# A chunked delta-rule scan in a DiT layer: whole Gram rows to memory, inverted blocks back in two transfers and spread on chip, key sums moved two chain steps up

## What is computed

```python
def update(s, w_t, k_t, v_t, kk_t, a_t):
    sa = jnp.einsum('ebhvk,ebhk->ebhv', s, kk_t)
    return s * w_t[..., None, :] - sa[..., :, None] * (kk_t * a_t)[..., None, :] + v_t[..., :, None] * k_t[..., None, :]

def rwkv_run_scan(s0, r, decay, k_dir, v, kk, a):
    ...
    s, y = wkv_scan(s0, per_dir(rw_heads(decay)), per_dir(rw_heads(k_dir)), shared(rw_heads(v)), shared(kk), per_dir(rw_heads(a)), rr)
    if y is not None:
        y = y[0] + jnp.flip(y[1], axis=1)
    return s, y
```

## Time and profile before

| | |
|---|---|
| median of three runs | 2519.59 us (2517.39 to 2519.63) |
| the profiled execution | 2521.18 us |
| its span in the profile | 2519.0 us |
| busy: PE, PEld | 2218.5 us (88%), 1843.3 us (73%) |
| busy: DVE, ACT, POOL | 938.4 us, 668.9 us, 877.0 us |
| DMA | 155526 packets, of which 103271 under 512 bytes |
| mean granted TensorE clock | 0.952 |

### The profile page before, as it was taken

How to read it: one execution, slowest core, us unless ns; L and a number is a source line. 1 busy time by engine, 2 the same in 40 slices (tenths; PEclk the granted TensorE clock), 3 DMA queues, 4 the chain that set the end, 5 groups by cost and what they waited for, 6 DMA issues and landing times. The chain is left out here.

```text
span 2519.0 us, 51099 instructions
## 1 busy us (share of the span) xinstructions
PE 2218.5 (88%) x22528; PEld 1843.3 (73%) x22528; DVE 938.4 (37%) x1467; ACT 668.9 (27%) x1027; POOL 877.0 (35%) x708
## 2 busy tenths in 40 slices
PE   5899989979699999999879996777777787999997
PEld 3787855655499999999729985666666665888785
DVE  3112265970500000122495126666666434000123
ACT  4111066421400000122222134444444313111112
POOL 2223200101143434434134454333333233666562
PEclk8999999989799999999889998999999988999998
DMA  6555520001022121121112342222222122232221
GB/s 254 204 209 193 216 93 18 1 34 50 17 67 67 58 66 58 58 68 59 44 67 75 105 145 55 45 46 45 45 45 43 27 73 80 95 97 92 92 92 67
DMA packets 155526, 205.64 MB, mean 82 GB/s; under 512 B 103271, under 2 KB 113767, under 8 KB 148168
## 3 DMA queue, kind: packets, MB, share of 16 engines
q1 hardware_dynamic: 155336, 202.78, 25.6%
HBM read 184.65 MB, written 18.09 MB: 80 GB/s over the span
## 5 line engine op out<-in xcount | busy, mean ns | idle before, releaser
L253 POOL CAST TMP_r<-WR 128x1024 fp32r<-128x1024 f32 x120 | 127.2, 1060 | 723.0 <-DMA WR<-in_ffn_w_dram 437.6
L272 PE MATMUL PS<-H_r,TMP_r 128*128 128x384 f32 (+1 forms) x1088 | 330.4, 359 | 11.0 <-DVE Y_r L489 11.0
L272 PE MATMUL PS<-Y_r,TMP_r 128*128 128x384 f32 (+1 forms) x1088 | 330.2, 358 | 3.7 <-DVE H_r L489 3.7
L255 POOL TENSOR_TENSOR WR_r<-WR,TMP_r 128x1024 fp32r<-128x1024 f32 x120 | 289.0, 2408 | 9.6
L412 DVE TENSOR_TENSOR P<-TMP,PS 128x768 f32 (+1 forms) x44 | 36.1, 821 | 562.5 <-PE PS L272 562.5
L272 PEld LDWEIGHTS PS<-H_r,TMP_r 128*128 128x128 f32 x1088 | 202.7, 190 | 27.5 <-DVE Y_r L489 11.7
L272 PEld LDWEIGHTS PS<-Y_r,TMP_r 128*128 128x128 f32 x1088 | 201.6, 190 | 19.3 <-DVE H_r L489 4.0
L272 PE MATMUL PS<-H_r,WR_r 128*128 128x384 f32 x736 | 191.9, 342 | 0.0
L395 ACT ACTIVATE TMP<-PS 128x768 f32<-128x768 f32 (+1 forms) x44 | 31.0, 705 | 526.0 <-PE PS L272 526.0
L589 PE MATMUL PS<-H_r,TMP_r 128*128 128x384 f32 x704 | 151.9, 338 | 3.2 <-DVE H_r L627 2.2
L272 PE MATMUL PS<-Y_r,WR_r 128*128 128x512 f32 x352 | 139.2, 396 | 0.0
(11 more groups left out here) (325 smaller groups left out, 4463.8 us busy)
## 6 DMA issues: line engine op xcount, KB each, us to landing
WR<-in_ffn_w_dram SPq DMA_DIRECT2D x88, 512.0 KB, 3.7
TMP<-in_mod_w_dram SPq DMA_DIRECT2D x40, 1024.0 KB, 5.0
WR<-in_down_dram SPq DMA_DIRECT2D x44, 512.0 KB, 3.5
WR<-in_mix_w_in_dram SPq DMA_DIRECT2D x24, 512.0 KB, 6.7
WR<-in_rw_w_rkv_dram SPq DMA_DIRECT2D x24, 512.0 KB, 4.4
P<-in_mod_w_dram SPq DMA_DIRECT2D x4, 2048.0 KB, 21.8
vkr_dram<-extra SPq DMA_DIRECT2D x16, 384.0 KB, 5.1
scan_front<-vkr_dram SPq DMA_DIRECT2D x16, 384.0 KB, 4.2
```

What stands on the lines that cost most here:

```text
L253: nc.gpsimd.tensor_copy(hi, raw).then_inc(weights_hi, 1)
L255: nc.gpsimd.tensor_tensor(lo, raw, hi.bitcast(F32), ALU.subtract).then_inc(weights_split, 1)
L272: last = nc.tensor.matmul(PS[:, bank + b, 0:h1 - h0], w, x[:, h0:h1], start=k + p == 0, stop=k == CT - 1 and p == 2)
```

## The change

1. Gram rows: 4 transfers (one for each direction and half of the partitions, whole rows of 64 values, 256 bytes) replace the 16 of L2109. They go to `gram_dram`, in which a chunk's matrix is followed by a gap of 64 values, so that the diagonal blocks of all 96 matrices lie at one stride; two transfers, one for each direction, read 16 values of each of 16 rows into each of 96 partitions.
2. Inverses: `XC` and `YC` come back dense, 128 partitions by 24 x 16 values, one transfer each. ACT spreads `XC` into the block-diagonal `XY` with 4 instructions whose scale is a column of `rowblock` (one for the partitions of that block, else zero), ahead of `ta`. DVE does the same for `YC`, 4 instructions ahead of `kin_0`. The fifth part still comes by 8 transfers, on a semaphore of its own. The solved rows and `XC`, `YC` share memory, so SP waits for `yt` of the round instead of for `tb`.
3. The sigmoid of the rate is no longer finished on POOL (`s01`, `s11` go): ACT reads the tanh, with the factor 0.5 moved into its column, and DVE adds 1 and multiplies by 0.5 within `ba` and `bt`, now scalar_tensor_tensor.
4. Order. PE: `kk` from between links 9 and 10 to between 7 and 8, `CK_0` and `KD_1` each one gap later, `kr` ahead of `CK_1`, `var` into the sweeps. ACT: `kc ksq` ahead of `tK_1`, `groot` ahead of `oo_0`, `vwide` ahead of `kT_0`. DVE: `kmax krec` between links 8 and 9, `m5` and `n_0` ahead of `f1 f2 z`, `kt_1` and `acc_1 accr` later in the chain, `kmul` ahead of the last masks.

```diff
-                        blocks = AM[:, n % 2, e].rearrange("p h j t -> p (h j) t")
                         for p in range(2):
-                            for b in range(4):
-                                at = 64 * p + BK * b
-                                sp.dma_start(blk_dram[e, :, p, b].rearrange("x s t -> s x t"),
-                                             blocks[at:at + BK, :, BK * b:BK * b + BK]).then_inc(blk_out, 16)
-                    sp.wait_ge(blk_out, 256 * n + 256)
-                    sp.dma_start(BLK.rearrange("q (e n) -> q e n", e=2),
-                                 blk_dram.rearrange("e x p b s t -> (x p b) e (s t)")).then_inc(blk_back, 16)
+                            sp.dma_start(gram_dram[e, :, p, 0:TC * TC].rearrange("x (s t) -> s x t", t=TC),
+                                         AM[H2[p], n % 2, e].rearrange("p h j t -> p (h j) t")).then_inc(blk_out[e], 16)
+                    for e in range(2):
+                        sp.wait_ge(blk_out[e], 32 * n + 32)
+                        diagonal = bass.AP(gram_dram.tensor, gram_dram[e].offset, [[BK * TC + BK, NBLK], [TC, BK], [1, BK]])
+                        sp.dma_start(BLK[:, BK * BK * e:BK * BK * (e + 1)].rearrange("q (s t) -> q s t", t=BK),
+                                     diagonal).then_inc(blk_back, 16)
...
-                        sp.wait_ge(pe_done, PEM["tb", i])
-                    for p, b in PB:
-                        sp.dma_start(XY[64 * p + BK * b:64 * p + BK * b + BK, 0:2, :, :, BK * b:BK * b + BK]
-                                     .rearrange("s a h j t -> s (a h j) t"),
-                                     inv_dram[0:2, :, p, b].rearrange("a x s t -> s (a x) t")).then_inc(x0_in, 16)
+                        sp.wait_ge(pe_done, PEM["yt", i])
+                    for k, dst, landed in ((0, XC, x0_in), (2, YC, y0_in)):
+                        sp.dma_start(dst, inv_dram[k:k + 2].rearrange("a x p b s t -> (p b s) (a x) t")).then_inc(landed, 16)
...
             def coupling(i):
                 b = back("ta", i)
-                pe.wait_ge(x0_in, 128 * i + 128)
+                pe.wait_ge(act_done, AC["xx", i])
...
                 if k == 1:
-                    pe.wait_ge(y0_in, 256 * i + 256)
+                    pe.wait_ge(dve_done, DV["yx", i])
...
                 if here(i):
+                    act.wait_ge(x0_in, 16 * i + 16)
+                    for b in range(4):
+                        last = nc.scalar.activation(XY[:, 0:2, :, :, BK * b:BK * b + BK].rearrange("p a h j t -> p (a h j) t"),
+                                                    XC, ACT.Copy, scale=ROWB[:, b:b + 1])
+                    AC.done(last, "xx", i)
                     coupled(i, "ta", TL[:, 0].rearrange("p h j t -> p h (j t)"))
...
-                DV.done(nc.vector.tensor_tensor(AA[e], KK, AA[e], ALU.mult), f"ba_{e}", n)
+                DV.done(nc.vector.scalar_tensor_tensor(AA[e], AA[e], 1.0, KK, ALU.add, ALU.mult), f"ba_{e}", n)
...
+                if here(i):
+                    v.wait_ge(y0_in, 16 * i + 16)
+                    for b in range(4):
+                        last = nc.vector.tensor_scalar(XY[:, 2:4, :, :, BK * b:BK * b + BK].rearrange("p a h j t -> p (a h j) t"),
+                                                       YC, ROWB[:, b:b + 1], None, ALU.mult)
+                    DV.done(last, "yx", i)
...
                     steps(i, 7, 8)
+                if here(c):
+                    v.wait_ge(act_done, AC["kroot", c])
+                    DV.done(nc.vector.tensor_scalar(KROOT, KROOT, 1e-12, None, ALU.max), "kmax", c)
+                    after("kmax", c)
+                    DV.done(nc.vector.reciprocal(KROOT, KROOT), "krec", c)
+                if here(i):
+                    steps(i, 9)
                 if here(n):
                     mask_rest(n, 0)
```

More of the change, by code:

```diff
@@ L1920, in hybrid_dit_kernel @@
         OO, TL, TX, UE = OOS[:, 0:4 * T], OOS[:, 0:2 * T], OOS[:, 2 * T:3 * T], OOS[:, 3 * T:5 * T]
+        XC, YC = (UE[:, k * 2 * NX * BK:(k + 1) * 2 * NX * BK].rearrange("p (x t) -> p x t", t=BK) for k in range(2))
         OO = OO.rearrange("p (e h j o t) -> p e h j o t", e=2, h=2, j=6, o=2)
@@ L2055, in projections_sp @@
                     next(scan)
+        H2 = [slice(0, 64), slice(64, 128)]
+        HQ = [(h, q) for q in range(2) for h in range(2)]
         PB = [(p, b) for p in range(2) for b in range(TC // BK)]
@@ L2208, in scan_pool @@
                             f"off_{e}", n)
-        H2 = [slice(0, 64), slice(64, 128)]
-        HQ = [(h, q) for q in range(2) for h in range(2)]
         def scan_pe(pe):
@@ L2453, in scan_pe @@
                     sweep(i, 1, 1)
+                    value_gram(i, 1)
                     sweep(i, 2, 0)
-                    value_gram(i, 1)
+                if here(i - 1):
+                    b = front("var", i - 1)
+                    pe.wait_ge(act_done, AC["sq", i - 1])
+                    PEM.done(turned_sums(b, FIN, 4), "var", i - 1)
+                if here(i):
                     sweep(i, 2, 1)
@@ L2553, in scan_pe @@
                 if here(i):
+                    chain(i, 8)
+                if here(n):
+                    gram_rest(n, 0)
+                if here(i):
+                    chain(i, 9)
+                if here(n):
+                    gram_keys(n, 1)
+                if here(i):
                     chain(i, 10)
-                if here(n):
-                    gram_rest(n, 1)
-                if here(i):
-                    outputs_carried(i)
                 if here(c):
@@ L2567, in scan_pe @@
                         yield
+                if here(n):
+                    gram_rest(n, 1)
+                if here(i):
+                    outputs_carried(i)
+                if here(c):
                     lora(c, 0)
@@ L2662, in scan_act @@
                                                  paired(front_bank("BV_1", i)), ACT.Copy), "bv_1", i)
+                if here(i - 1):
+                    act.wait_ge(pe_done, PEM["var", i - 1])
+                    AC.done(nc.scalar.activation(VROOT, PS[:, front_bank("var", i - 1), 0:8], ACT.Sqrt, scale=1.0 / CH,
+                                                 bias=small[:, 3:4]), "groot", i - 1)
                 if here(n):
@@ L2685, in scan_act @@
                                                  VROOT.unsqueeze(2).broadcast_to([128, 8, TC]), ACT.Copy), "vwide", i - 1)
+                if here(n):
+                    turned(n, 0)
                 if here(n):
@@ L2714, in scan_act @@
                         yield
+                if here(n):
+                    tokens(n, "tK_1", TOKK[:, 1])
                 if here(c):
@@ L2917, in scan_dve @@
                 if here(n):
+                    decayed(n, 0)
+                if here(i):
+                    states(i, 1)
+                if here(n):
+                    queries(n, 1)
                     direct(n, 1)
+                if here(i):
+                    after("n_1", i)
+                    steps(i, 1)
+                if here(n):
                     decayed(n, 1)
                 if here(i):
-                    states(i, 1)
-                    after("n_1", i)
-                    steps(i, 1)
+                    steps(i, 2)
                 if here(n):
@@ L2942, in scan_dve @@
                 if here(i):
-                    steps(i, 9)
+                    steps(i, 10)
                 if here(n):
                     mask_keys(n, 1)
-                if here(i):
-                    steps(i, 10)
+                if here(c):
+                    v.wait_ge(pe_done, PEM["kr", c])
+                    DV.done(nc.vector.tensor_tensor(as_halves(KK), as_halves(KK), halves(front_bank("kr", c)), ALU.mult),
+                            "kmul", c)
                 if here(n):
@@ L2954, in scan_dve @@
                           .then_inc(input_split, 1)
-                if here(c):
-                    v.wait_ge(act_done, AC["kroot", c])
-                    DV.done(nc.vector.tensor_scalar(KROOT, KROOT, 1e-12, None, ALU.max), "kmax", c)
-                    after("kmax", c)
-                    DV.done(nc.vector.reciprocal(KROOT, KROOT), "krec", c)
-                if here(c):
-                    v.wait_ge(pe_done, PEM["kr", c])
-                    DV.done(nc.vector.tensor_tensor(as_halves(KK), as_halves(KK), halves(front_bank("kr", c)), ALU.mult),
-                            "kmul", c)
                 if here(i):
```

83 lines of the change are left out of this document (31 added, 52 removed), and 29 rows, old and new, of tables (AC, DV, PEM).

## The result

Against a forecast of 2510 us, the changed kernel is slower: 2534.87 us in the median of six executions against 2519.61 before, ratio 1.0059 with an interval of 1.0039 to 1.0079. One of the six took 12051 us and counts in no comparison; the other five (2526.29 to 2544.4) have a median of 2532.23. The loss is about 15 us, and the time lies outside the range of 2489 to 2524.5.

What follows compares the result with a forecast made beforehand. POOL's late loop through memory was taken to set the round's end. Six full rounds (−1.2), the last (−6) and the first (−2.5) sum to −9.7 us, from 2519.6 to 2510; own range 2498 to 2514.5, overall 2489 to 2524.5.

Steps and rivals of the forecast that it cites:

- What bounds the kernel: End of the round: POOL, late through the loop through memory, holds kmax; PE then waits 2.3 for kwide and 1.09 for kmul.
- at most 1.5 us a round for one stop: Middle: one PE stop of 1.5 us may move with PE's instruction count and take back part of the removed gaps.
- The Gram transfers, "6 us earlier": Gram rows out and back: first issue to POOL's substitution takes 9.2 us instead of 15.4; bounds 2 to 7.4 earlier.
- `kmax`, "+1.4": Behind link 8 in the chain: kmax waits for POOL's clearing, +1.4 us a round; bounds 0.2 and 4.1.
- The sum 6.0 − 6 + 2.0 − 0.9: Link 8 to POOL's end: old distance, POOL earlier, middle's gain, late keys; it leaves 1.1 us of waiting for kmax.
- the rivals of no change and of slower: Gram transfers give less, so kmax is held longer: no change, 4.5 us, 2519, chance 0.23; slower, 3.0 us, 2526, chance 0.15.
- The chain, "+0.9" and "+1.4": Links at the end of the round: +0.9 us for kk waiting on late keys, +1.4 for kmax waiting on POOL.
- The tail's removed waits, "−3.4 + 0.9": End of the round: PE's waits for kwide and kmul go, −3.4 us; CK_1 waits for a mask pair, +0.9.
- The head, "+2.0": Head of a round: ta waits for ACT's spread, 4.0 us later, less u1_0's saved wait; net +2.0, bounds 1.1 and 4.0.
- The middle, "−2.0": Middle of a round: m5 and n_0 pass the wait for vr, closing gaps ahead of n_1, yt and first link; −2.0 us.
- the 3.5 beyond the 2.0: Middle: at most 3.5 us a round could go; all of it would, if instruction refills were mostly hidden.
- The ends: Last round: −6 us, from earlier inverses and its middle; first round: −2.5, from its kwide wait less a loss in the head.

Runs made afterwards that it cites:

- Run d: The kernel before with the new Gram transfers alone (4 out, 2 back); 0.9975 of the kernel before.
- Run i: The changed kernel with one more wait on POOL, so that off_0 and off_1 start only after krec; 0.9997 of the kernel before.
- run m: Run l without POOL's wait for krec; 0.9968 of the kernel before.
- run b: The changed kernel with the old order of PE and DVE steps at the end of the round; 1.0061 of the kernel before.
- run e: The kernel before with only m5 and n_0 put ahead of f1 f2 z on DVE; 0.9992 of the kernel before.
- f: The changed kernel with the old order at the end of the round and both spreads early; 0.9982 of the kernel before.
- g: The kernel before with the new Gram transfers and m5 and n_0 ahead of f1 f2 z; 0.9947 of the kernel before.
- Run l: Run i with XC spread by ACT between the first tanh pair and sq, and YC behind cen; 0.9891 of the kernel before.
- Run a: The changed kernel with XC spread ahead of the copy of ys and YC ahead of cen; 0.9975 of the kernel before.
- run n: Run i with acc_1 and accr ahead of kt_1 on DVE, so the keys load earlier; 0.9985 of the kernel before.

## Why the prediction was wrong, by its own steps

**What bounds the kernel: right as far as it goes.** POOL's loop through memory set the end of the round. Run d shows it: the transfers alone free `kmax`, the stretch from the last state to the last tanh falls from 13.6 to 11.5 us, and the round is shorter. It was not the only bound. I looked for waits, and the waits went; two other things came up in their place. Over the six rounds from `ta` to `ta`, added up from the traces (idle is time in which neither a matmul nor a weight load ran; both are counted as PE instructions):

| | before | after |
|---|---|---|
| PE idle just ahead of every 256th PE instruction | 27.6 us | 37.5 us |
| PE idle elsewhere | 40.7 us | 20.5 us |
| time at the lower clock level | 22.4 us | 58.2 us |

The other idle time fell by 20 us, the new wait at `ta` included, as the change was meant to do. The stops of the earlier trace rows took 10 of them back, and 36 us more were spent at 1.2 GHz instead of 2.4, half of them between `ta` and `u1_0` and nearly half in links 7 to 10. My sum had at most 1.5 us a round for one stop and nothing for the clock.

**The Gram transfers, "6 us earlier": the start right, the end wrong.** I had 9.2 us to the first substitution and it came at 9.0. But I moved its end by the same 6 us. It lasts 18.1 instead of 15.5, so the gain at POOL's end was 3.1 us (mean of five rounds, from `mA_0` to the end of `off`: 35.9 before, 32.8 after). Taking for each of the 30 instructions its shortest time in the scan, they sum to 10.9 us in both kernels; what they take beyond it rose from 2.6 to 4.8 us. The stretched ones lie over DVE instructions that take both inputs from SBUF: 57 of the 150 in five rounds, against 32 before. Two of POOL's instructions of one size, and the DVE instruction that lay over most of each, with one input from PSUM (0.38 us) and with both from SBUF (1.01 us):

```profile
1707.39 0.38 POOL L2194 TENSOR_TENSOR scan_small<-scan_small 96x110 f32<-96x110 f32 x1
1706.99 0.68 DVE L2925 TENSOR_TENSOR hyc<-PS,scan_front 128x512 f32<-128x512 f32 x1
1707.85 1.01 POOL L2195 TENSOR_TENSOR scan_small<-scan_small 96x110 f32<-96x110 f32 x1
1707.59 1.00 DVE L2805 TENSOR_TENSOR scan_front<-scan_front 128x768 f32<-128x768 f32 x1
```

A duration that holds at one place in the round was carried to another.

**`kmax`, "+1.4", is the step that failed.** The sum 6.0 − 6 + 2.0 − 0.9 had POOL 6 us earlier. With the 3.8 of the round shown (30.9 − 27.1) it gives 3.3, and the four rounds that were held show 2.5 to 3.6 in `kmax`. It is what I had as the rivals of no change and of slower, whose point was POOL's transfers giving 3.0 to 4.5 instead of 6; they gave what I said, but the substitution took it back. Run i prices it at 16 us, run m at 19. By the Trainium skill, "SBUF — State Buffer", section "SBUF: two separate sides", GpSimd and some VectorE operations lock the same pair of ports, and whichever comes second is blocked for the other's whole instruction. By that rule, the runs i and m agree, with `kmax` at 164 ns and 2575 ns. The traces show more: every held `kmax` ends within 0.04 us of the second of POOL's two instructions, though in the changed kernel it started during the first, or 0.02 us ahead of it.

**The chain, "+0.9" and "+1.4": too little, and the clock left out.** The whole chain from link 1 to the last state takes 15.8 us against 12.4 (mean of five rounds), +3.4, where my terms for keys and `kmax` made +2.3. With the hold away, in run i, it is still +1.4, of which 1.0 lies between link 1 and link 7. In the new order the clock falls whether `kmax` is held or not. In the six rounds that have a `kk` (the five above and the one ahead of them), links 7 to 10 ran at a clock of 1.00 in all 36 windows of the six kernels with the old order (before, b, d, e, f, g), and at 0.61 to 0.80 in 38 of 60 windows of the ten with the new one. In 26 of these 38 `kmax` was not held (under 0.9 us). Run l pays it in five rounds of six, and its links 7 to 10 take 5.9 to 6.4 us there and 4.9 in the other. So the clock is a price of the new order and not of the stall. No run here has run l's spreads with an order that keeps the clock.

**The tail's removed waits, "−3.4 + 0.9": a little less.** From the last state to the last tanh it is 1.9 us shorter, not 2.5. `CK_1` waits for its masks, as I said, 0.70 in the round shown.

**The head, "+2.0": right in mechanism, mis-sized.** The spread takes 2.12 us (I had 2.1) and `ta` comes 3.9 us later against the last tanh in every round (4.0). But less came back at `u1_0`: from `ta` to `u1_0` it is 5.4 us before and 4.5 after in the mean of the six full rounds, 0.9 saved and not 2.0. Net +3.0. Run a prices the place at 21 us, with its new wait in it; run l against run i at 27.

**The middle, "−2.0": the size right, the cause not shown.** From the end of `u1_0` to link 1 it is 33.4 us before and 31.3 after (mean of five rounds). One stop of 1.17 us stands where waits were, and none of the 3.5 beyond the 2.0 came. But the edit that I put this down to gave 0.8 alone (run e, from the start of `u1_0`) and 0.1 beside the transfers (g against d); `var`, `groot` and `vwide` were moved in the same stretch, and no run takes them apart. By the Trainium skill, "Runtime: NRT & Kernel Launch", section "Instruction fetch mechanics", instructions are refilled in blocks of 256 and the crossing is mostly hidden. By that rule, the trace of the changed kernel disagrees again: the stops of over 1 us that nothing in the program ends stand at multiples of 256 PE instructions from one another, and of the 77 such places in the six full rounds PE idles over 0.2 us at 36 (23 before).

**The ends: the last round right, the first wrong.** −6 was forecast for the last round, and −7.4 came. For the first I had −2.5; from the first `l00` to the second `ta` it is 6.1 longer, since both losses act there too. That is 8.6 us of the 21 by which the scan missed the sum.

In sum: per full round −2.0 (middle) + 3.0 (head) + 3.4 − 1.9 (chain and tail) = +2.5 instead of −0.2; the rounds measured from `ta` to `ta` are 2.1 longer.

## What to carry to other kernels

When a long instruction of POOL is moved, look up which small instructions of DVE it will now lie over, and where those stand: 0.16 us that becomes 2.8 costs 16 to 19 us inside a chain that PE follows. One wait on POOL, for something it does not need, was the cheapest repair.

Two repairs that don't add up need not be one cause: look for the wait that the first repair made. And an instruction added to a queue is costed by what stands behind it: the dense return with its spreads was worth −0.45% or +0.6% by their place alone.

A wait removed is not yet time gained. Add up what PE does in a whole round, idle time by kind and the granted clock, before and after: here half of the removed waits came back as stops with no releaser, and the clock was lower for 36 us more.

## What the runs showed of the hardware

The order of small steps on PE can cost clock: links 7 to 10 ran at 1.00 in the kernel before and at 0.71 to 0.72 in all five rounds of run n, where PE is busy 27.61 us of 29.76 and `kmax` is not held. Before the falls of the changed kernel PE had waited 0.8 to 1.2 us for `kk` and run its 12 matmuls of two columns; in the kernel before, `kk` stands behind link 9 and the clock stays. Whether `kk`'s place is the cause was not tried.

The stops of the earlier trace rows stand at every 256th of PE's instructions, weight loads and matmuls both counted, at the same count in all 16 kernels. They last up to 2 us, and at half of these places or more there is none. Run l has 42.2 us of them in six rounds, more than the kernel before with 27.6, though its other waits are half as long.

The same substitution on POOL took 15.8 or 17.9 us (means of five rounds) by what DVE did meanwhile, with the same 10.9 us of shortest times. In before and after, POOL's instructions were stretched by 0.2 to 0.6 us each where they lay mostly over DVE instructions with both inputs in SBUF, and by under 0.01 us over those with an input in PSUM.

Stretches in which nothing was changed differ between the profiled executions, one of each kernel: the stretch ahead of the scan (to the start of the first `l00`) took 1471.3 to 1478.0 us, the one behind it 470.2 to 474.6. Whether that goes with the execution or with the kernel is open. A difference of 5 us in one span is therefore not a result here; the parts have to be compared. Timed ratio and profiled scan can part by more than that: run b is 15 us slower than before by its ratio and 3.5 us longer in the scan of its trace, run d 6 us faster and 13.8 us shorter.
